# Taking the idle matrix products out of a two-block transformer kernel on one core

## The reference, cut to what matters

```python
def route(h, w_router, b_router):
    probs = jax.nn.softmax((h @ w_router).astype(jnp.float32), -1)
    sel = probs + b_router.astype(jnp.float32)
    ...                       # best group of four experts, best two in it
    return expert, gate

def expert_block(args):       # for each block of packed tokens
    xblk, e = args
    return (jax.nn.silu(xblk @ w_gate[e]) * (xblk @ w_up[e])) @ w_down[e]
```

## Time and profile before

| | |
|---|---|
| three runs | 2072.03 us median (2062.91 to 2074.38) |
| the profiled execution's own time | 2067.21 us |
| its span in the profile | 2065.5 us |
| PE busy | 1760.3 us, 85% |
| identity products (L132) | 160 records |
| mean granted clock of PE | 0.938 |

### The profile page before, as it was taken

One profiled execution on the slowest core, in us unless ns is written; L12 is line 12 of the kernel. 1 busy time (PEld: TensorE's weight loads), 2 busy tenths in 40 slices (PEclk: granted clock), 3 DMA queues, 4 the chain that ended last, 5 costly groups with the idle time before them and its releaser, 6 DMA issues. The chain is left out here.

```text
span 2065.5 us, 23444 instructions
## 1 busy us (share of the span) xinstructions
PE 1760.3 (85%) x9328; PEld 910.0 (44%) x9328; DVE 773.3 (37%) x1888; ACT 423.3 (20%) x995; POOL 289.4 (14%) x284
## 2 busy tenths in 40 slices
PE   9999996776655556668999999988799999999986
PEld 7779873552321111124564444333377543443332
DVE  3955177776667777854230000000213300000002
ACT  2481122221221112223121110000124200010001
POOL 0000033443444444440000000000000000000000
PEclk9999998998887776689999999999999999999999
DMA  7237389999999999997799999999944999999997
GB/s 269 90 128 298 143 351 387 399 421 421 421 421 421 421 421 421 421 421 293 323 383 428 426 426 428 426 427 425 422 204 172 410 427 426 428 426 426 427 426 297
DMA packets 79263, 761.81 MB, mean 369 GB/s; under 512 B 8661, under 2 KB 9654, under 8 KB 17703
## 3 DMA queue, kind: packets, MB, share of 16 engines
q1 hardware_dynamic: 41478, 489.34, 56.7%
q0 software_dynamic: 37664, 270.84, 31.9%
HBM read 759.10 MB, written 1.05 MB: 368 GB/s over the span
## 5 line engine op out<-in xcount | busy, mean ns | idle before, releaser
L2640 PE MATMUL bank<-arena 128*64 128x512 f32 x3072 | 679.5, 596 | 47.6 <-DMA arena<-in_w_up 20.1
L1085 PE MATMUL bank<-arena 64*64 64x512 f32 x2032 | 321.1, 785 | 226.1 <-ACT arena L795 226.1
L2640 PEld LDWEIGHTS bank<-arena 128*64 128x64 f32 x3072 | 232.6, 137 | 480.6 <-issue 460.5
L1458 DVE CUSTOM_DVE_ANT_0 arena<-arena 128x1024 f32<-128x1024 f32 x256 | 313.7, 1225 | 159.2 <-DMA arena<-in_peer_uv,arena 155.7
L588 POOL DMA_INDIRECT arena<-in_peer_uv,arena x256 | 278.2, 1087 | 627.6 <-PE bank L1085 308.0
L2767 DVE TENSOR_TENSOR arena<-arena,bank 128x512 f32<-128x512 f32 x32 | 22.0, 688 | 708.1 <-PE bank L2640 708.1
L1085 PEld LDWEIGHTS bank<-arena 64*64 64x64 f32 x2032 | 92.5, 176 | 434.0 <-ACT arena L795 257.8
L844 PE MATMUL bank<-arena 128*128 128x272 f32 (+2 forms) x768 | 144.8, 349 | 0.2 <-ACT arena L614 0.2
L844 PEld LDWEIGHTS bank<-arena 128*128 128x128 f32 x768 | 126.2, 191 | 19.4 <-issue 2.5
L790 ACT ACTIVATE arena<-arena 128x4 f32<-128x4 f32 (+1 forms) x69 | 14.1, 205 | 467.2 <-DVE arena L1458 467.2
L1541 POOL DMA_DIRECT2D arena<-in_w_router x2 | 1.1, 573 | 556.6 <-POOLq L2525 522.0
(11 more groups left out here) (458 smaller groups left out, 1482.3 us busy)
## 6 DMA issues: line engine op xcount, KB each, us to landing
arena<-in_w_up SPq DMA_DIRECT2D x64, 2048.0 KB, 36.4
arena<-in_w_down SPq DMA_DIRECT2D x64, 2048.0 KB, 37.1
arena<-in_w_gate SPq DMA_DIRECT2D x64, 2048.0 KB, 32.4
arena<-in_w_in SPq DMA_DIRECT2D x13, 2048.0 KB, 8.3
arena<-in_w_out SPq DMA_DIRECT2D x2, 4096.0 KB, 18.2
arena<-in_wq SPq DMA_DIRECT2D x3, 2048.0 KB, 12.7
arena<-in_rg_out SPq DMA_DIRECT2D x2, 2048.0 KB, 11.4
arena<-in_peer_uv,arena POOLq DMA_INDIRECT x256, 17.4
```

What stands on the lines that cost most here:

```text
L1085: m = pe.matmul(bank[banks[t][half]][to:to + HALF, :], DIAG[lo:lo + HALF, k + j, :], row[lo:lo + HALF, D + half * 512:D + (half + 1) * 512 ...
L1458: v.tensor_tensor_reduce(SLOT[slot_of[j]][:, 0:D] if n == 0 else SCR, SLOT[slot_of[j]][:, 0:D], XF[u // PH], 1.0, 0.0, ALU.mult, ALU.add, ...
L2640: x = pe.matmul(bank[b][j * C:(j + 1) * C, :], operand[:, c, j * C:(j + 1) * C], RING[s % AHEAD][:, c % (DC // 2), j, :], start=(c == 0), ...
```

## The change

The helper `keep_busy` and its three calls go. The field `idle_bank` of the router stays, unused. Nothing else is changed; no wait is added or taken away.

```diff
-def keep_busy(pe, bank, ident, n):
-
-    for _ in range(n):
-        pe.matmul(bank[:, 0:P], ident, ident, start=True, stop=True)
...
                     if u * R + k == LAST:
-                        keep_busy(pe, bank[6], ident, 8)
                         te.wait_ge(s_diag, LAST + 2)
                         last_sums(u, k)
...
             m.then_inc(self.s_mm, 1)
-        keep_busy(pe, K.bank[self.idle_bank], K.ident, 32)
+
         te.wait_ge(self.s_vec, CHOSEN)
...
-            keep_busy(pe, bank[0], ident, 4)
+
             visits(te, visit, lambda m: pack(m, m * 2, m * 2), visit_last)
```

## The result

The changed kernel is slightly slower. Its median is 2071.49 us (20 runs, 2069.47 to 2077.19) against 2069.11 us (20 runs, 2062.06 to 2074.38); the ratio is 1.0022, with a 95% interval of 1.0014 to 1.0030: 4.6 us of 2069.11, between 2.9 and 6.2.

A forecast was written before the change was run, and what follows sets the result against it. Weight transfers are at their limit, but the stream hangs on PE's first step in each expert stage. Two routers at 1.1 + 2.2 = 3.3 us, other products 0, give 6.6 us more: 2076 us, range 2067 to 2086.

The forecast's parts named there:

- The gate: Expert stages: PE's first step releases the first waiting weight load; time lost before it delays the end, later losses are absorbed.
- The fall in the idle time: Both routers: without the 32 products PE idles some 7.8 us ahead of the ranks, and its clock falls to 0.50.
- Ranks, 1.1 us: Each router: the ten rank records run at half clock, 1.1 us more (bounds nothing and 1.15), all landing on the path.
- `pack` and first step, 2.2 us: Start of each expert stage: both start cold until the clock returns, costing 2.2 us (1.4 to 3.0).
- Rival 1: Expert stages: the clock returns only in the steps, all of `pack` cold; 14 us in all, 2084 us; chance 0.17.
- Last sums, 0: Last sums, without their eight products: a cold stretch is covered by the wait for weights; 0 (bounds 0 and 1.8 us).
- Rival 4: Last sums in `front_stage`: low clock through all of them adds 1.8 us to the forecast, 2078 us; chance 0.10.
- Rival 2: Expert stages: transfers absorb the delay, or ranks and `pack` are not slowed; nothing arrives at the end, 2070 us; chance 0.10.
- rival 3: Start of expert stages: without the four products each starts 0.26 us earlier if the clock stays up; 2069 us; chance 0.03.
- The forecast 6.6 us: Whole kernel: slower by 6.6 us, 3.3 us for each of two routers and 0 elsewhere (2.8 to 8.3).
- The four products, taken at 0: Ahead of each expert stage: `pack` waits for DVE anyway, so removal gains at most 0.1 us a stage; taken as 0.

The follow-up runs named there:

- a known delay of 2.86 us: The kernel before with 48 identity products in each router instead of 32; ratio 1.0044 (1.0028 to 1.0060).
- the run of its own: The kernel before with only the 8 identity products ahead of the last sums taken out; ratio 0.9996 (0.9986 to 1.0006).
- the four products' own run: The kernel before with only the 4 identity products ahead of each expert stage taken out; one profile, distances of 25.63 and 25.60 us.
- the late delay: The kernel before with 16 more identity products in the fourth pair of each expert stage, behind turn_pack; ratio 1.0011 (1.0001 to 1.0021).
- the end of layer 0: The kernel before with 24 more identity products at the end of layer 0's expert stage; ratio 1.0008 (0.9997 to 1.0019).

## Why the prediction held, step by step

**The gate.** The end of an expert stage hangs on PE's first step: held. The distance from first load to end stayed (435.58 and 435.42 us), a known delay of 2.86 us ahead of it was paid, a later one was mostly absorbed.

**The fall in the idle time:** held. The clock was at 0.50 when the ranks began in all four routers of the changed kernel; in two it fell in the idle time, in two before it.

**Ranks, 1.1 us:** held, 1.0 us in all four routers of the changed kernel.

**`pack` and first step, 2.2 us (1.4 to 3.0):** held. The four routers of the changed kernel have +2.92, +1.58, +1.67 and +2.99 us, 2.3 us in the mean. Rival 1 (3.7 + 2.2 us) is out: the clock comes back within `pack` in all four, 3.3 to 6.2 us behind its start, where I had 2.7 to 6.

**Last sums, 0:** held; in the profile of the changed kernel the 1.7 us fell into the wait for the weights. Rival 4 (1.8 us) is out by that trace, and by the interval of the run of its own, which ends at 1.2 us. **Rival 2** (absorbed) is out by the interval, and **rival 3** by the four products' own run.

**Where the sum was wrong.** The forecast 6.6 us lies above the measured interval of 2.9 to 6.2 us. Three things, with both signs:

1. *"They begin at 1611.34 ..., the granted clock now stays at 1.00."* I took the loss to start in the idle time. It can start before, in the logits: +1.06 and +0.75 us in one profile of the changed kernel, nothing in the other, 0.45 us a router in the mean.
2. *The four products, taken at 0.* They are not without effect. With them alone taken out, the clock fell at the start of `pack` in both routers, at a cost of 1.6 us each. Of the fifteen routers that kept these four behind ranks at full clock, it fell between ranks and `pack` in three. That they help the clock over the thin stretch from ranks to `pack` fits this, but the two routers are of one profile, so it is not shown. Without the 32, the clock is down already. Then the four delay `pack` by 0.9 us, and `pack` and the first step are shorter by as much (8.8 us in the mean of two routers, 9.7 in the mean of four without them). Leaving the logits' share out, the distances are 27.2 us with the four and 27.3 without. So 0 stands as the net of this change, as two effects that cancel and not as nothing.
3. *The kernel before as a fixed 24.0 us.* That was its profile, not its average. Ten routers have been profiled with all identity products around them as before (the kernel before twice, and the runs with the late delay, the last sums and the end of layer 0): seven took 23.96 to 24.01 us, three took 24.87, 26.51 and 28.05. Their mean is 24.7 us. The four of the changed kernel (28.98, 27.29, 26.67, 27.94) have 27.7 us. The difference, 3.0 us a router, 6.0 us in all, is near my 6.6 partly by luck: the first point, which I had not foreseen, adds 0.45 us a router, and this one, which I had not foreseen either, takes off 0.7. The timed 4.6 and 4.1 us (2.9 to 6.2 and 1.9 to 6.4) agree with 6.0 only at their upper end; with ten and four routers for the means I can't tell whether the rest is chance. That a change under 0.5% could not be told from none was also wrong: with twenty runs of each kernel the interval is 0.08% wide to either side.

The forecast time of 2076 us was 4.5 us high: 2 us from the size of the effect, and the rest because the kernel before has a median of 2069.11, not 2069.6, and the changed one a smaller median than its ratio suggests (2.4 us apart, where the ratio gives 4.6).

## What to carry to other kernels

Products that nobody reads pay for themselves where what follows them decides the end; here that was the step that frees the first slot of a ring, not the 90% of the stage behind it. Look for that gate, not for the engine with the largest share. And a granted clock of 1.00 in one profile is one execution: filler kept the clock up here in most routers, but where the clock has fallen ahead of it, the filler itself runs at half speed and becomes the delay. Compare several profiles of the same stretch before calling it hidden.

## What the runs showed of the hardware that was not expected

- A fully busy PE can lose its clock. PE was fully busy with records of 128 x 16, and the granted clock fell to 0.50 in them; with twice as many it fell in both routers. What part the turning ahead of them has is open.
- Whether it fell in the single logits differed from one execution to the next of the same instructions: in 9 of the 26 routers profiled with them it fell in them or within 0.2 us of their end, seven of these in layer 0. The logits took 3.64 us in some routers, 3.81 to 4.71 in others.
- An idle time of 2.25 us followed by ten narrow records was enough for a fall within these, where the ranks behind some 0.5 us of idle time kept the clock in all twelve routers that have this. But with 2.99 us of idle time ahead of the last sums it stayed at 1.00 in one execution, and 2.77 us ahead of them were followed by a fall in both profiles of the changed kernel. The length of the idle time alone does not decide it.
- Transpositions did bring the clock back. In the second profile of the changed kernel PE was idle for 5.89 us, then did nothing but turn the result, and the clock was back at 1494.2, 0.5 us before the turning ended:

```profile
1491.38 3.34 PE L2700 MATMUL bank<-ident,h_res 128*128 128x128 f32 x16 [5.89 <-DVE h_res L2789]
```

```profile
1493.00:1494.00 1.00, 1.00 (x7) 0.50 0.89 352
1494.00:1495.00 1.00, 0.72 (x5) 0.88 1.06 426
```

In the kernel before, the same transpositions had not done so the earlier trace rows, and I had taken that as the rule of the Trainium skill (TensorE: Matmul & The Clock Gate, Part 4), by which transpositions do not count as work for the clock. The other profiles speak against it. In twelve of the fourteen the clock fell ahead of this turning; in seven of these it came back before PE did anything else than turn, and in five only 4.0 to 4.8 us into the next stage. So transpositions can bring it back, and whether they do differed between executions of the same stretch. Here the measurement decides. The prediction had no row of this when it weighed rival 1.
